# Finishing tokens inside the expert stage: scatter of first visits, gather, add, norm and scatter of last visits

## The reference, cut to what matters

```python
out = lax.map(run_block, (row_tok.reshape(n_blk, MOE_BLOCK), blk_e)).reshape(n_blk * MOE_BLOCK, D)
y = jnp.zeros((N, D), jnp.float32).at[st].add(out[dest].astype(jnp.float32) * sw[:, None])
...
hp = hp + hier_moe(rms_norm(hp, norm_ffn_g[l]), *moe_args)
...
y_prompt = rms_norm(hp, final_norm_g)
y_sample = rms_norm(hs, final_norm_g)
```

## Time and profile before

| | us |
|---|---|
| median of 3 runs (lowest, highest) | 1158.72 (1155.5, 1158.74) |
| span of the profiled execution | 1155.7 |
| PE busy | 1069.8 (93%) |
| DVE busy | 570.3 (49%) |
| ACT busy | 411.5 (36%) |
| POOL busy | 242.8 (21%) |
| expert stage, first transposes to the end of the last down products | 743.3 to 1122.4 |
| from there to the end of the span | 33.3 |

### The profile page before, as it was taken

How to read it: one execution, slowest core, us unless ns; L and a number is a source line. 1 busy time by engine, 2 the same in 40 slices (tenths; PEclk the granted TensorE clock), 3 DMA queues, 4 the chain that set the end, 5 groups by cost and what they waited for, 6 DMA issues and landing times. The chain is left out here.

```text
span 1155.7 us, 16387 instructions
## 1 busy us (share of the span) xinstructions
PE 1069.8 (93%) x6188; PEld 722.9 (63%) x6188; DVE 570.3 (49%) x1275; ACT 411.5 (36%) x973; POOL 242.8 (21%) x298
## 2 busy tenths in 40 slices
PE   6999999999998999999998998799999999999980
PEld 3643324554455677777786555486878787878760
DVE  4406699999988876666845641313111111111114
ACT  2325533978354455556531343111111111111114
POOL 4731116644411000000005110011212121212110
PEclk9999999999997999999998899899999999999995
DMA  8600000000192310111011771499999999999928
GB/s 267 229 18 1 1 18 1 9 30 5 41 246 91 125 56 27 48 38 56 27 60 64 279 284 69 157 367 344 328 335 344 333 345 334 340 337 342 278 33 318
DMA packets 51342, 191.42 MB, mean 166 GB/s; under 512 B 10926, under 2 KB 13950, under 8 KB 41029
## 3 DMA queue, kind: packets, MB, share of 16 engines
q1 hardware_dynamic: 39583, 142.71, 34.7%
q0 software_dynamic: 11536, 47.71, 14.6%
q10 hardware_dynamic: 158, 0.16, 0.1%
HBM read 162.49 MB, written 28.19 MB: 165 GB/s over the span
## 5 line engine op out<-in xcount | busy, mean ns | idle before, releaser
L1542 PEld LDWEIGHTS ps<-mem 128*128 128x128 f32 x2048 | 235.3, 193 | 16.8 <-issue 16.8
L1542 PE MATMUL ps<-mem 128*128 128x96 f32 x2048 | 234.8, 276 | 0.8 <-DVE mem L2538 0.8
L1618 ACT ACTIVATE mem<-ps 128x512 f32<-128x512 f32 (+7 forms) x338 | 149.4, 482 | 227.3 <-PE ps L1338 58.9
L2102 DVE TENSOR_SCALAR_CACHE_REDUCE mem<-mem 128x768 bf16<-128x768 f32 (+2 forms) x134 | 166.5, 1284 | 0.0
L1383 PE MATMUL ps<-mem 128*128 128x256 f32 (+1 forms) x544 | 125.5, 383 | 2.3 <-DVE mem L2391 1.3
L1548 PE MATMUL ps<-mem 128*96 128x512 f32 x256 | 119.3, 609 | 2.5 <-DVE mem L2530 2.5
L2530 DVE TENSOR_TENSOR mem<-mem,ps 128x192 f32<-128x192 f32 x32 | 11.4, 355 | 211.6 <-ACT mem L1978 211.6
L1383 PEld LDWEIGHTS ps<-mem 128*128 128x128 f32 (+1 forms) x544 | 98.8, 187 | 18.8 <-DVE mem L2402 2.6
L1021 POOL DMA_INDIRECT h_rows<-mem x32 | 46.5, 1454 | 296.6 <-DVE mem L2545 296.6
L1978 ACT ACTIVATE mem<-ps 128x192 f32<-128x192 f32 x32 | 10.6, 331 | 261.2 <-PE ps L1542 261.2
L1548 PEld LDWEIGHTS ps<-mem 128*96 128x96 f32 x256 | 39.5, 164 | 58.3 <-issue 52.4
(11 more groups left out here) (306 smaller groups left out, 1442.6 us busy)
## 6 DMA issues: line engine op xcount, KB each, us to landing
mem<-in_expert_w_gate SPq DMA_DIRECT2D x32, 1024.0 KB
mem<-in_expert_w_up SPq DMA_DIRECT2D x32, 1024.0 KB
mem<-in_expert_w_down SPq DMA_DIRECT2D x32, 1024.0 KB
mem<-in_x_prompt SPq DMA_DIRECT2D x16, 512.0 KB, 4.1
mem<-in_w_in SPq DMA_DIRECT2D x3, 2048.0 KB, 9.9
h_rows<-mem SPq DMA_DIRECT2D x8, 512.0 KB, 2.6
xn_rows<-mem SPq DMA_DIRECT2D x8, 512.0 KB, 2.9
mem<-h_rows SPq DMA_DIRECT2D x8, 512.0 KB, 5.4
```

The source lines that it names most:

```text
L1542: ins = mm(ps[:, 2 + s, j * CAP:(j + 1) * CAP], wgu[w][:, j // 2, k, (j % 2) * P:(j % 2 + 1) * P], xgT[:, s, k, :], start=(k == 0), stop=( ...
L1618: return fn(out, in_, ACT.Copy, scale=scale)
L2102: v.tensor_scalar(bufs[a % 3][0:R, 0:w], sc, mid[:, a:a + 1], None, ALU.is_ge, ALU.add, accum_out=cnt[:, a:a + 1]).then_inc(step, 1)
```

## The change

There is no accumulating DMA and no pass over the table at the end any more. Of a token's two visits, the one at the lower expert number is its first and the other its last (a visit in the overflow counts as behind all experts). Expert by expert:

- The output rows `ob` of first visits are scattered to a new table `first_expert_rows`; rows that don't take part get a row number beyond the table, and the DMA's bounds check leaves them out (`slot_first`, `FAR_ROW`).
- For last visits POOL gathers the row from that table into `rg` and the residual row from `h_rows` into `hg` (`slot_last`); DVE adds the three (`sum_up`); ACT squares and roots (`spread`); DVE norms (`norm_out`); POOL scatters the result to the two outputs (`finished`; `slot_late` is for the sample tokens).
- The four steps are spread over the loop: in the step of expert e POOL issues the scatter and the gathers of e and the output scatters of e-2, DVE does `sum_up(e-1)` and `norm_out(e-2)`, ACT `spread(e-2)`.
- To tell first from last, the token number in the slot matmul carries a quarter (`TV`, made by `later_ones` from ranks and experts), and `targets()` takes number and quarter apart. Token numbers now count down, so that an empty slot is beyond the table.
- SP clears all of `first_expert_rows` ahead of the prompt's tiles (nine DMAs) in place of the padding rows. The final norm's weights are loaded at the start of the stage. The loop at the end goes.

```diff
+            for i in range(TILES):
+                sp.dma_start(rowsof_dram(r_dram, i).rearrange("p (c n) -> p c n", n=P),
+                             zrow[0:rows(i)].unsqueeze(1).broadcast_to([rows(i), D // P, P])).then_inc(first_cleared, 16)
...
+            def gathered(rows_, src, table, e, last_row, done):
+                pool.indirect_dma_start(rows_, None, src, bass.IndirectOffsetOnAxis(ap=table[0:CAP, e:e + 1], axis=0),
+                                        bounds_check=last_row, oob_is_err=False).then_inc(done, 16)
...
-                add_rows(e, ob[0:CAP, e % 2, :], eo_out[e % 2])
+                scattered(r_dram, slot_first, e, NTOK - 1, ob[0:CAP, e % 2, :], eo_out[e % 2])
                 if e:
                     pool.wait_ge(eo_out[(e - 1) % 2], 16 * ((e - 1) // 2 + 1))
+                if e >= 2:
+                    pool.wait_ge(fin_ready, e - 1)
+                gathered(rg[0:CAP, e % 2, :], r_dram, slot_last, e, NTOK - 1, rg_in[e % 2])
+                if e >= HRING:
+                    pool.wait_ge(y_out[e % HRING], 32 * (e // HRING))
+                gathered(hg[0:CAP, e % HRING, :], h_dram, slot_last, e, NTOK - 1, hg_in[e % HRING])
+                if e >= 2:
+                    finished(e - 2)
...
+            def spread(e):
+                s = e % 2
+                act.wait_ge(fin_ready, e + 1)
+                if e >= 2:
+                    act.wait_ge(y_ready, e - 1)
+                fn(sq[0:CAP, :], hg[0:CAP, e % HRING, :], ACT.Square, accum_out=ssq3[0:CAP, s:s + 1]).then_inc(ssq3_ready, 1)
+                act.wait_ge(ssq3_ready, e + 1)
+                fn(std3[0:CAP, s:s + 1], ssq3[0:CAP, s:s + 1], ACT.Sqrt, scale=1.0 / D, bias=const("eps", CAP)).then_inc(std3_ready, 1)
...
-                for n in range(2):
-                    link(v.tensor_scalar(token_hot_s[n], OH[0:r, n, :], const("tokid", r)[:, i:i + 1], None, ALU.mult))
                 take(dve, "2b", "M", t)
                 rank(i)
...
+                later_ones(slice(i, i + 1), r, 2)
+                for n in range(2):
+                    v.tensor_scalar(token_hot_s[n], OH[0:r, n, :], TV[0:r, n, i:i + 1], None, ALU.mult)
...
+            def sum_up(e):
+                out, s = hg[0:CAP, e % HRING, :], e % 2
+                for c in range(2):
+                    dve.wait_ge(dn_emptied[c], e + 1)
+                dve.wait_ge(hg_in[e % HRING], 16 * (e // HRING + 1))
+                dve.wait_ge(rg_in[s], 16 * (e // 2 + 1))
+                link(v.tensor_tensor(out, out, rg[0:CAP, s, :], ALU.add))
+                v.tensor_tensor(out, out, ob[0:CAP, s, :], ALU.add).then_inc(fin_ready, 1)
+
+            def norm_out(e):
+                out, s = hg[0:CAP, e % HRING, :], e % 2
+                dve.wait_ge(std3_ready, e + 1)
+                link(v.reciprocal(rstd3[0:CAP, s:s + 1], std3[0:CAP, s:s + 1]))
+                v.scalar_tensor_tensor(out=out, in0=out, scalar=rstd3[0:CAP, s:s + 1], in1=gb[0:CAP, :],
+                                       op0=ALU.mult, op1=ALU.mult).then_inc(y_ready, 1)
...
             def experts(q, last=False):
                 for u in range(WSLOTS):
+                    e = q * WSLOTS + u
                     gate(q, u)
                     if u < WSLOTS - 1 or not last:
                         keep_xgT(q, u + 1) if u < WSLOTS - 1 else keep_xgT(q + 1, 0)
+                    if e == NE - 1:
+                        sum_up(e - 1)
+                        norm_out(e - 2)
                     keep_out(q, u)
+                    if 1 <= e < NE - 1:
+                        sum_up(e - 1)
+                    if 2 <= e < NE - 1:
+                        if e == 2:
+                            dve.wait_ge(gn_in, 16)
+                        norm_out(e - 2)
```

More of the change, by code:

```diff
@@ L574, in program @@
                     filled[tag + q], emptied[tag + q] = filled[before], emptied[before]
-                    seen[q] = use[before[:1]][before[1:]]
+                    tag_before = "2a" if before[:2] == "2a" else "1"
+                    seen[q] = use[tag_before][before[len(tag_before):]]
                 else:
@@ L2248, in _, with later_ones @@
             dve.wait_ge(init_done, 5)
+            def later_ones(tiles, r, ks):
+                ef, rk, key, later = (x[0:r, tiles, :] for x in (EF, RK, KEY, LATER.unsqueeze(2)))
+                link(v.tensor_scalar(key, rk, float(CAP), float(NE), ALU.is_ge, ALU.mult))
+                link(v.tensor_tensor(key, key, ef, ALU.add))
+                link(v.tensor_tensor(later, key[:, :, 1:2], key[:, :, 0:1], ALU.is_gt))
+                ids, late = const("tokid", r)[:, tiles], LATER[0:r, tiles]
+                v.scalar_tensor_tensor(out=TV[0:r, 1, tiles], in0=late, scalar=-0.25, in1=ids, op0=ALU.mult, op1=ALU.add)
+                v.tensor_scalar(TV[0:r, 0, tiles], late, 0.25, -0.25, ALU.mult, ALU.add)
+                dve.drain()
+                link(v.tensor_tensor(TV[0:r, 0, tiles], TV[0:r, 0, tiles], ids, ALU.add))
             def route(i):
@@ L2598, in _ @@
             experts(NE // WSLOTS - 1, last=True)
+            sum_up(NE - 1)
+            norm_out(NE - 2)
+            norm_out(NE - 1)
             for s in range(2):
                 dve.wait_ge(eo_out[s], 16 * (NE // 2))
+            for s in range(HRING):
+                dve.wait_ge(y_out[s], 32 * (NE // HRING))
             dve.wait_ge(dest_ready, 1)
```

190 lines of the change are left out of this document (112 added, 78 removed).

## The result

The changed kernel takes 1197.3 us (median of 4 runs, 1195.35 to 1199.41) against 1158.73 for the kernel before beside it: ratio 1.0334, 95% interval 1.0314 to 1.0353. The forecast was 1155.1, in a range of 1149 to 1172. The profiled execution has a span of 1193.1 us (1155.7 before) in a time of 1195.35, so there are 37.4 us to explain. All ratios leave out executions that took over 1.5% more than the fastest of the same kernel; this changes one figure only, the ratio of run 12.

A forecast was written before the change was run, and what follows sets the result against it. TensorE was taken to set the expert step, 11.6 us, with head and tail uncovered. Tail -9.7, head +1.7 and expert 3 +4.4 sum to -3.6: span 1152.1, time 1155.1 us, range 1149 to 1172.

The forecast's parts named there:

- Steady steps: One expert step: stays at 11.6 us at no cost if POOL keeps up, rows landing within the time allowed.
- Rival E: Expert steps: rows land later than the 10 us allowed, TensorE waits in most steps, about 1175 us; chance 0.07.
- GpSimd, prices: POOL's DMA issues: 1.3 us taken for each, between bounds 1.23 and 1.76; six per expert.
- Rival C: POOL's queue in every step becomes the bound past 1.93 us mean spacing: 1167 us at 2.0, 1201 at 2.2; chance 0.14.
- D: Rival: in each step VectorE's two-SBUF-input operations and POOL's DMA instructions shut each other out, +20, 1175 us; chance 0.07.
- VectorE and ScalarE in the step: Added work fits idle time: VectorE 4.0 of 6.7 us free, ScalarE 4.2 of 8.15 idle; no cost.
- Expert 3: Overflow destinations behind expert 3's multiply: adds, norm and small operations lengthen TensorE's wait, +4.4 us (3.0 to 6.5).
- Head: Ahead of the first gather: more small VectorE operations in the chain, +1.7 us (0.9 to 2.0).
- Tail: After TensorE's end: reload, nine norms and nine stores go, one chain for expert 31 stays, -9.7 us.
- Rival B: Tail gives back only 1 to 6 us, bounds-checked scatters costing what the scatter-add does; 1158.5 us (1157 to 1164), chance 0.20.
- The ninefold clear: SP's clear ahead of the prompt's tiles: 7.5 us of issue, hidden by 41 us, no cost.

The follow-up runs named there:

- run 12: Kernel before with three more gathers an expert behind the scatter-add, all their rows skipped: 1174.73 us, ratio 1.010.
- run 4: Changed kernel with the gathers of residual and first-expert rows issued ahead of the wait for the expert's output and its scatter: 1185.75 us, ratio 1.026.
- run 13: Kernel before with one more gather of 96 real token rows an expert, into a buffer nobody reads: 1198.13 us, ratio 1.034.
- run 5: Changed kernel with the experts interleaved (0, 8, 16, 24, 1, 9, ...) instead of in natural order: 1195.02 us, ratio 1.033.
- run 3: Changed kernel without each expert's second output scatter (the sample output, mostly skipped rows): 1189.12 us, ratio 1.027.
- run 10: Changed kernel without the loads of down weights from expert 4 on, all row transfers kept: 1165.46 us, ratio 1.005.
- run 14: Changed kernel with GpSimd and VectorE waiting for the output scatters' landing inside the overflow branch, not ahead of its register load: 1190.93 us, ratio 1.028.
- run 9: Kernel before with the overflow destinations cut in three pieces behind experts 3, 4 and 5: 1155.75 us, ratio 0.9981.
- run 8: Kernel before with the overflow destinations computed behind the last expert's output instead of behind expert 3: 1159.02 us, ratio 1.000.
- run 7: Changed kernel with four token buffers, residual and first-expert gathers ahead of the scatter, destinations last and experts interleaved: 1187.49 us, ratio 1.024.
- run 11: Kernel of run 7 with ScalarE taking Identity in place of Sqrt, sparing both table loads a step: 1173.67 us, ratio 1.014.

## Why the prediction was wrong, point by point

- **Steady steps, the step that failed first of all.** "The step holds at 11.6", because the token gather starts 7.3 to 8 us behind a multiply, may take 9.8 to 10.5 to land, and "the longest landing is 9.9". Both halves failed in the four steps where TensorE waited. The gather started 8.9, 9.4, 9.4 and 11.0 us behind the multiply, and landed 9.3, 12.5, 13.7 and 9.1 later (up to 17.8 in run 4). It starts late since the residual rows land late: VectorE waits for them, 37.2 us in all, behind it the norm is late, GpSimd waits with its output scatters for the norm, and the next token gather stands behind those. For the rows of expert 10, timeline of the changed kernel:

```profile
860.19 1.22 DVE L2619 TENSOR_TENSOR mem<-mem 96x1024 f32<-96x1024 f32 x1 [2.25 <-DMA mem<-h_rows,mem]
864.89 0.94 POOL L1015 DMA_INDIRECT out<-mem  x1 [2.60 <-DVE mem L2627]
867.37 0.98 POOL L1011 DMA_INDIRECT mem<-xn_rows,mem  x1 [0.30 <-issue]
```

  The 9.9 was of a queue with two transfers a step; six stand in it now. "Bytes: 96 rows gathered and 96 added become 68 + 4 x 34, so the queues get no more" is wrong by its own sum, 204 rows for 192, and the queue moves 1.6 MB more. The window with a DMA share of 1.02 was read as "the engines are busy too" and not as "there is no room" (run 13: one more gather, +40 us). The mean of 34 last visits hid that a token's two experts lie in one group of eight: experts 7, 15 and 23 have 68, 56 and 80, the first of each group, 8, 16 and 24, none, and the waits stand around the end of a group (run 5 moves them). And of 576 row slots a step 372 are skipped (by the routing of the inputs), each a packet (runs 3, 12). The Trainium skill (DMA: Bandwidth & Descriptors, "Queues, rings and completion order") has each DMA engine take turns between the queues it has work for, a packet at a time; that a gather without bytes took 9.6 us to land beside the weights (run 12) agrees. Together the steps cost 17.7 us for token rows. Rival E named this, at 0.07 and 1175.
- **GpSimd, prices.** Right: 1.23 to 1.29 apart, as in 870.78, 872.01 and 873.30. Bounds-checked DMAs cost GpSimd 0.93 to 0.98 each. Rival C is wrong. D's mechanism exists after all, at a price that no step's length shows (last section).
- **VectorE and ScalarE in the step.** The durations are right (two additions and links 2.5, square and root as given), and run 10 shows they cost nothing. What the forecast missed is the late silu, 5.2 us behind steps 18 and 30 and another 1.9 us in step 5: "the Silu's load waits only for the expert two steps back, so it is over before the products are". It is over, at 4.2 us ahead of the last product, and the silu is late all the same.
- **Expert 3, +4.4 forecast, +8.8 measured.** The wait was to be 6: it is 5.7 in runs 4 and 10, where steps 4 and 5 cost 4.0 and 4.1 us more than before, but 8.30 in the changed kernel, 2.5 of it for late residual rows, and the silu of step 5 adds its 1.9. So this part was right, and the rest is again late rows and a late silu.
- **Head, +1.7 forecast, +3.7 measured.** The first gather starts 2.9 later (741.80 for 738.88). The six operations and the second pair of products cost 1.3; VectorE comes to them 1.0 later, perhaps since the same operations for the prompt's tokens were not hidden (no run shows it); and GpSimd starts 0.84 us behind VectorE's last operation, not 0.27. TensorE's first product and the gap ahead of it add 0.9 (9.70 for 9.10, 1.17 for 0.82). The start of the stage varies between executions by more than this cost: 754.3 to 758.0 in the runs of the kernel before, 754.6 to 760.0 in those of the changed one.
- **Tail, -9.7 forecast, +0.4 measured: the other step that failed.** The chain was right up to the last issue: 20.0 us behind TensorE's end for a forecast of 18.2 (issue at 1179.28, end of products 1159.30). The landing was shorter than forecast, at most 2.8 for 5.4. But the sum ends there, and puts what follows at nothing: register load and branch, 3.6 us, and GpSimd's drain with the closing, 7.4 us. In the kernel before they were hidden beside the pass over the table, which the change takes away. So 1.8 more up to the issue, 2.6 less for the landing and 11.0 for the rest make the 10.1 us that are missing, but for rounding. Rival B isn't borne out: it had dearer scatters, and these are 1.22 apart. 7.4 and 5.4 us of the tail could be had (runs 4 and 14).
- **The ninefold clear** shows in no wait, as forecast. Sum of the measured terms: 3.7 + 8.8 + 17.7 + 5.2 + 1.5 + 0.4 = 37.3, or 37.4 before rounding. Most of the steps' part has one cause, loaded DMA engines: with a third less weights (run 10) the 31 steps take 7.7 us over 11.60 each, with all of them 36.8, and 3.5 in the kernel before.

The last norms and scatters of the changed kernel; timelines:

```profile
1172.84 1.28 DVE L2627 SCALAR_TENSOR_TENSOR mem<-mem 96x1024 f32<-96x1024 f32 x1
...
1174.47 1.28 DVE L2627 SCALAR_TENSOR_TENSOR mem<-mem 96x1024 f32<-96x1024 f32 x1
```

```profile
1174.93 1.60 POOL L1015 DMA_INDIRECT out<-mem  x1 [6.69 <-DVE mem L2627]
1176.84 0.92 POOL L1015 DMA_INDIRECT out<-mem  x1 [0.30 <-issue]
1178.06 0.91 POOL L1015 DMA_INDIRECT out<-mem  x1 [0.30 <-issue]
1179.28 0.92 POOL L1015 DMA_INDIRECT out<-mem  x1 [0.30 <-issue]
```

Four scatters stand in a row, since GpSimd takes those of expert 30 only behind VectorE's last additions.

## What to carry to other kernels

Where the DMA engines' share is at 1 beside a full TensorE (1.02 here), price an added transfer by what it does to the landing of the transfers behind it, not by its issue: count packets, the skipped rows among them, and count them for the worst step, not for the mean. A landing time read from a queue with two transfers a step doesn't hold for six. When a change takes work away from the end of a kernel, look for what ran hidden beside it, in the views of the sequencers too and not only in the timeline. And when a stall of an auxiliary computation costs a few microseconds, cutting it in pieces that fit the idle time of each step (run 9) can be worth more than moving it elsewhere (run 8).

## What the runs showed of the hardware

- A row that the bounds check skips moves no bytes but takes a packet: 96 rows and 16 more for each transfer, in runs 3 and 12 (112 and 336 a step). Hardly any of its cost is the engines' own time: by the packet records of run 12, the small packets of the software queue from 860 to 980 us took 11 ns each, 1.9% of the 16 engines' time, and yet a gather of nothing but such rows took 9.6 us to land.
- A silu can start late behind a table load that is over. In run 7 ScalarE idled 5.8 to 5.9 us behind the load in 15 steps, and 4.2 to 5.3 in the others from step 4 on, where the silu followed the last product by 0.3 us or less. No such wait is left without the table switch (run 11), nor with the switch and a third less weight traffic (run 10, against three in the changed kernel). So it takes both, the switch and loaded DMA engines; what is fetched or waited for stays open. The Trainium skill (ScalarE: Activation LUTs, "What ACT_TABLE_LOAD costs") gives 1283 ns and a drain of about 1380; the load is 1283 here too, in steps with the delay and without it, and this delay of 1.6 to 1.7 us, in some steps only, is none of the two.
- GpSimd's drain at the end of its list took 7.1 us in the changed kernel whether the last rows had landed (1185.7, changed kernel) or not (1183.0, run 14), 5.3 in the kernel before, 4.3 in run 3 and 3.5 in run 12. What sets its length stays open.
- VectorE's operations with two SBUF inputs do hold up GpSimd's DMA issues, now and then. Of the 192 issues of the stage 14 took 1.2 to 1.9 us in place of 0.9 to 1.0, and each of the 14 ran beside such an operation; 68 others ran beside one too, 52 of them for over 0.3 us, and were not held up. The other traces agree: over both kernels and all runs 157 issues took 1.2 us or more (scatter-adds not counted), every one beside such an operation, and of the 1453 issues beside none the longest took 1.01. What else it takes stays open; with a third less weights it was 2 of 93 (run 10). VectorE lost nothing. In the timeline of the changed kernel:

```profile
873.15 1.22 DVE L2619 TENSOR_TENSOR mem<-mem 96x1024 f32<-96x1024 f32 x1 [3.22 <-DMA mem<-h_rows,mem]
874.40 1.23 DVE L2620 TENSOR_TENSOR mem<-mem 96x1024 f32<-96x1024 f32 x1
```

```profile
872.01 0.98 POOL L1011 DMA_INDIRECT mem<-first_expert_rows,mem  x1 [0.30 <-issue]
873.30 1.92 POOL L1011 DMA_INDIRECT mem<-h_rows,mem  x1 [0.31 <-issue]
```

  The Trainium skill (SBUF — State Buffer, "Who interferes with whom") has such operations contend with a GpSimd instruction that reads SBUF, and tells of a probe in which they did not stall descriptor generation. Here some issues were stalled, by up to 0.9 us.
- A wait of TensorE can cost up to twice its length. Step 23 had 2.23 us of it, and steps 23 and 24 took 4.2 us over 11.60 each: the down projection behind the wait took 5.30 us for 3.67, at a mean granted clock of 0.68. Of the seven waits over 1.5 us in the steps, five were followed by such a slow one (4.6 to 5.6 us, 0.65 to 0.77), two, of 1.86 and 1.59, by one of 3.67 at 1.00. The lower of the two levels is the 0.50, or 1.2 GHz, that the earlier trace rows shows.
- What stays open: how the 17.7 us divide between skipped rows and added real transfers. Taking a quarter of the skipped rows away (run 3) did not shorten TensorE's stage; adding 288 a step to the kernel before made it some 17 us longer, but with a later issue of the token rows (run 12), so neither run gives the share.
